# Adaptive modulation by channel tile, with the first two tiles of h in three pieces

## What is computed

```python
def rms_norm(x, g):
    xf = x.astype(jnp.float32)
    y = xf * lax.rsqrt(jnp.mean(xf * xf, axis=-1, keepdims=True) + RMS_EPS)
    return (y * g.astype(jnp.float32)).astype(x.dtype)
...
    c_act = jax.nn.silu(c)
...
        mod = (c_act @ w_ada[l] + b_ada[l])[:, None, :]
        shift, scale, gate = jnp.split(mod, 3, axis=-1)
        h = rms_norm(x, g_norm[l]) * (1 + scale) + shift
        proj = h @ w_in[l]
...
        x = x + gate * (m @ w_out[l])
```

## Time and profile before

| | us |
|---|---|
| median of 3 runs (918.33 to 919.73) | 918.34 |
| span of the profiled execution | 917.1 |
| TensorE busy | 902.9 (98%) |
| VectorE busy | 797.5 (87%) |
| ScalarE busy | 414.1 (45%) |
| GpSimd busy | 100.7 (11%) |

### The profile page before, as it was taken

The page is one execution under the profiler, slowest core; times in us unless marked ns, Lnnn a source line. Parts: engine busy times, 40 slices in busy tenths (PEclk is TensorE's granted clock), DMA queues, the critical chain, the costliest instruction groups (busy, mean ns, idle before and its releaser), DMA issues.

```text
span 917.1 us, 17124 instructions
## 1 busy us (share of the span) xinstructions
PE 902.9 (98%) x7004; PEld 884.6 (96%) x7004; DVE 797.5 (87%) x915; ACT 414.1 (45%) x582; POOL 100.7 (11%) x109
## 2 busy tenths in 40 slices
PE   8999999999999999999999999999999999999996
PEld 5699999999999999999999999999999989999996
DVE  1797999997999996999997799999798798689767
ACT  5484354434453443454433445446434432436452
POOL 0122211111110201211111203000011000000000
PEclk9999999999999999999999999999999999999998
DMA  9879989889798979798888989648897662522515
GB/s 367 348 175 224 258 207 255 226 224 245 200 227 248 256 236 236 195 249 243 250 253 251 229 234 226 201 139 291 350 343 184 194 252 90 155 74 92 164 68 185
DMA packets 86366, 202.75 MB, mean 221 GB/s; under 512 B 12433, under 2 KB 19089, under 8 KB 82833
## 3 DMA queue, kind: packets, MB, share of 16 engines
q1 hardware_dynamic: 52960, 122.76, 38.7%
q0 software_dynamic: 22080, 52.46, 28.5%
q10 hardware_dynamic: 11248, 26.45, 8.1%
HBM read 175.67 MB, written 88.88 MB: 288 GB/s over the span
## 4 chain that ended last, share of the span: by engine, by line
PE 95%; DMA 2%; DVE 1%; SPq 1%; issue 0%; ACT 0%; DVEq 0%
PE ps L1080 23%; PE ps L1076 23%; PE ps L1074 23%; PE ps L1011 8%; PE ps L1014 8%; PE ps L1012 8%; DMA ada_raw<-w_ada 2%; PE ps L941 1%; PE ps L993 1%; PE ps L947 0%; PE ps L1272 0%; PE ps L1270 0%; PE ps L1269 0%; DVE bf L1821 0%; DVE hf L2374 0%
## 5 line engine op out<-in xcount | busy, mean ns | idle before, releaser
L2012 DVE SCALAR_TENSOR_TENSOR conv_y<-conv_u,par_all,conv_y 128x1024 f32<-128x1024 f32 x240 | 301.1, 1284 | 2.1 <-DVE conv_y L1998 0.6
L1076 PE MATMUL ps<-tr,hr 128*128 128x258 f32 x824 | 216.4, 283 | 0.0
L1074 PE MATMUL ps<-tr,hr 128*128 128x258 f32 x824 | 215.4, 283 | 0.0
L1466 ACT ACTIVATE hr<-raw 128x512 fp32r<-128x512 f32 (+1 forms) x188 | 115.9, 618 | 116.1 <-PE ps L1080 87.5
L1080 PE MATMUL ps<-tr,hr 128*128 128x258 f32 x824 | 166.4, 283 | 0.0
L1076 PE MATMUL ps<-hr 128*128 128x258 f32 x616 | 161.5, 283 | 0.0
L1074 PE MATMUL ps<-hr 128*128 128x258 f32 x616 | 160.8, 282 | 0.0
L1074 PEld LDWEIGHTS ps<-tr,hr 128*128 128x128 f32 x824 | 156.9, 190 | 0.0
L1076 PEld LDWEIGHTS ps<-tr,hr 128*128 128x128 f32 x824 | 155.7, 189 | 0.0
L1891 DVE TENSOR_TENSOR hr<-raw,hr 128x512 fp32r<-128x512 f32 (+1 forms) x188 | 126.5, 677 | 5.5 <-ACT hr L1466 1.6
L1080 PEld LDWEIGHTS ps<-tr,hr 128*128 128x128 f32 x824 | 127.3, 188 | 0.0
(11 more groups left out here) (289 smaller groups left out, 1581.5 us busy)
## 6 DMA issues: line engine op xcount, KB each, us to landing
w_sums<-w_main POOLq DMA_DIRECT2D x64, 512.0 KB, 9.5
raw<-w_sums SPq DMA_DIRECT2D x120, 256.0 KB, 4.5
raw<-w_main SPq DMA_DIRECT2D x94, 256.0 KB, 4.8
w_sums<-w_sums POOLq DMA_DIRECT2D x30, 512.0 KB, 5.8
w_sums<-w_main ACTq DMA_DIRECT2D x26, 512.0 KB, 5.5
ada_raw<-w_ada SPq DMA_DIRECT2D x8, 1024.0 KB, 21.1
w_raw<-w_main SPq DMA_DIRECT2D x16, 512.0 KB, 5.7
bf<-x_t SPq DMA_DIRECT2D x4, 1032.0 KB, 8.1
```

What stands on the lines that cost most here:

```text
L1074: nc.tensor.matmul(bank[:, c, :], wh[:, w_cols], x_hi[:, k, t_cols], start=start and k == 0, stop=False, skip_group_check=True)
L1076: nc.tensor.matmul(bank[:, c, :], wh[:, w_cols], x_lo[:, k, t_cols], start=False, stop=False, skip_group_check=True)
L1466: nc.scalar.activation(ring(q)[0][:, 0:n], raw5[:, raw_slot(q), 0:n], ACT.Copy).then_inc(item_hi, 1)
L2012: ins = v.scalar_tensor_tensor(out=y, in0=conv_u[:, x, k:k + SEQ], scalar=par_all[:, g, x, k:k + 1], in1=y, op0=ALU.mult, op1=ALU.add)
```

## The change

- **Modulation by tile.** w_ada's shift and scale columns are stored as 8 blocks of 256 columns, one for each channel tile (the gate's two blocks become the tensor w_gate). There are 8 products, 8 row copies of 256 columns and 8 turns of two matmuls, in place of 4 of each of double size. VectorE's modulation is two instructions of 9 columns, straight from the PSUM bank, and uses scale_b = (1 + b_scale) * g_norm, which is made once at the start.
- **Squares.** ScalarE squares tiles 0, 2, 4, 6 and half of 7, VectorE tiles 1, 3, 5 and the other half. TensorE sums eight strips of 129 columns on eight groups of 16 rows, so that the root and the reciprocal have 129 columns in place of 258. The last two tiles of x are loaded apart.
- **h.** VectorE first multiplies x by the spread 1/rms in place (x_norm; from tile 2 on x_norm_row with the copied row), ScalarE then makes the full h with scale and shift (h_full) and copies it to the high part (h_hi), and VectorE subtracts (h_lo, a plain subtraction). Tiles 0 and 1 go in pieces of 387, 387 and 258 columns, and TensorE's step of job 0 on them waits for piece after piece (split_step).
- **Order.** c's SiLU and its table come at ScalarE's start. The first w_ada block and its product come before the first weights and the spreading. Jobs 0 and 1 go in turn for 6 tiles in place of 5. Fewer spare matmuls.

```diff
-QCOLS = TOK // QUADS
+PIECES = 2 * QUADS
+PCOLS = TOK // PIECES
+PIECE_BANKS = [(0, 3), (3, 6), (6, PIECES)]
+H_PIECES = [slice(p0 * PCOLS, p1 * PCOLS) for p0, p1 in PIECE_BANKS]
+SPLIT_TILES = 2
-WARM_SPREAD = 5
+WARM_SPREAD = 3
-WARM_TURN = 3
-WARM_FIRST = 4
+WARM_TURN = 1
...
-            for n in range(4):
-                sp.dma_start(bf[:, 2 * n:2 * n + 2, :], t["x_t"][:, 2 * n:2 * n + 2, :]).then_inc(x_loaded[n], 16)
+            for n, rows in enumerate([slice(0, 2), slice(2, 4), slice(4, 6), slice(6, 7), slice(7, 8)]):
+                sp.dma_start(bf[:, rows, :], t["x_t"][:, rows, :]).then_inc(x_loaded[n], 16)
...
+            for e in range(1, KT):
+                sp.dma_start(ada_raw[:, e, :, :], t["w_ada"][e]).then_inc(ada_loaded[e - 1], 16)
...
-            together = KT - 3
+            together = KT - 2
...
+            for k in range(2, together):
+                first_steps(k, [0])
+                if k + 2 < KT - 1:
+                    turn(k + 2)
+                if k + 3 < KT:
+                    ada(k + 3)
+                first_steps(k, [1])
+                if k == KH:
+                    turn(KT - 1)
...
+            for e in range(1, KT, 2):
+                dve.wait_ge(x_loaded[x_load(e)], 16)
+                columns = slice(HALF, TOK) if e == KT - 1 else slice(0, TOK)
+                v.tensor_tensor(hf[:, e, columns], bf[:, e, columns], bf[:, e, columns], ALU.mult).then_inc(x_squared_dve, 1)
+                if e == 1:
+                    dve.wait_ge(small_loaded, 64)
+                    link(v.scalar_tensor_tensor(out=scale_b.rearrange("p (q x) -> p q x", x=2), in0=ada_b[:, 0:PAIRS, 2:4], scalar=1.0,
+                                                in1=vecs[:, G_NORM, :].rearrange("p (q x) -> p q x", x=2), op0=ALU.add, op1=ALU.mult))
...
+            for e in range(1, KT):
+                modulation(e)
+                h_samples(e)
+                if e + 1 < KT:
+                    x_norm_row(e + 1)
+                h_lo(e)
+                if e == 3:
+                    first_split(0, 1)
+                    first_split(1, 1)
```

More of the change, by code:

```diff
@@ new lines, in square_sums @@
+            def square_sums(e):
+                for h in range(2):
+                    picked = pick_half[:, h * QUAD // 2:h * QUAD // 2 + QUAD]
+                    for g in range(QUADS):
+                        quad = slice(g * QUAD, (g + 1) * QUAD)
+                        p = 2 * g + h
+                        last = nc.tensor.matmul(x_sums[quad, :], picked, hf[:, e, p * PCOLS:(p + 1) * PCOLS], start=(e == 0 and h == 0),
+                                                stop=(e == KT - 1 and h == 1), tile_position=(0, g * QUAD))
+                return last
@@ L991, in token_sums, with spread_rstd @@
+            def spread_rstd(b):
+                p0, p1 = PIECE_BANKS[b]
+                for p in range(p0, p1):
+                    row = p * QUAD // 2
+                    last = nc.tensor.matmul(rstd_bank[b][:, (p - p0) * PCOLS:(p - p0 + 1) * PCOLS], eye[:, row:row + 1].broadcast_to([P, P]),
+                                            x_rstd, start=True, stop=True)
+                last.then_inc(x_spread, 1)
             def token_sums(out, row, done):
@@ L1424, in _ @@
+            h_full(1, 0)
+            ada_out(2)
+            h_full(1, 1)
+            h_hi(1, 0)
+            h_full(1, 2)
+            h_hi(1, 1)
+            h_hi(1, 2)
+            ada_out(3)
+            for e in range(SPLIT_TILES, KT):
+                h_full(e, 0)
+                h_hi(e, 0)
+                if e + 2 < KT:
+                    ada_out(e + 2)
+                if e == 3:
                     first_split(0, 1)
                     first_split(1, 1)
-                if e % 2 == 1 and e > 1:
-                    h_full(e - 3)
-                    h_full(e - 2)
@@ L1429, in _ @@
-            h_full(KT - 2)
-            h_full(KT - 1)
             def evac_first(s):
@@ L1833, in _ @@
[L1833 to L1841 removed]
+            for b in range(len(H_PIECES)):
+                x_norm(1, b)
+            for e in range(1, KT):
[4 more added lines that the diff above has]
+                h_lo(e)
+                if e == 3:
```

311 lines of the change are left out of this document (172 added, 139 removed).

## The result

The changed kernel takes 927.7 us (median of 4 runs, 925.4 to 930.0) where the kernel before takes 918.6 on the same chip (4 runs, 918.3 to 919.7): a ratio of 1.0091, with a 95% interval of 1.0069 to 1.0113. It is slower, by 8.4 us by the ratio (9.1 by the medians), with an interval of 6.3 to 10.4. The forecast was 926.0 in a range of 921.0 to 929.6. The profiled execution is the slowest of the four; its own time is 930.0 and its span 928.2. The spans of the four are 928.2, 924.5, 923.6 and 927.3, 925.9 on the mean, against 925.1 in the sum.

A forecast was written before the change was run, and what follows sets the result against it. TensorE's stream was taken to bound the kernel: span 917.1 + 5.5 (job 2's shift) + 2.5 (clock) = 925.1 us, plus 1.2 from span to median, 926.3, given as 926.0. Range 921.0 to 929.6.

The forecast's parts named there:

- Part 1: Squares: VectorE waits for the small tensors, eye at 13.7 us, holding later squares and TensorE's sums; +3.55 us.
- Part 2: From root to first step: halved columns and pieces start the first step at 28.5 us, 2.9 earlier than before.
- Part 3: Tiles of h: a chain between VectorE and ScalarE takes 3.9 us a tile; TensorE waits 2.5 us before step 7.
- Part 4: Ahead of job 2: TensorE waits 1.4 us for VectorE's weight split; job 2 at 67.05, shift +5.5 us without the clock.
- Part 5: TensorE's clock falls to half at idle gaps ahead of sum 3, the first step and around step 7; +2.5 us, bounds 0 and 4.9.
- a sign of being wrong: TensorE showing a wait behind 70 us that it didn't have before would prove the prediction wrong.
- the measure: Start of job 2, 61.55 us before: its shift was taken as the shift of the whole kernel.
- The clock holds: Rival: no half-clock stretch ahead of or behind sum 3; 923.8 us, or 923.0 with h_full at 1.15; chance 0.17.
- VectorE isn't held: Rival: eye lands before tile 3's square needs it, sums keep their old pace; some 919.8 us; chance 0.05.
- The ring is shorter: Rival: a tile of h takes 3.2 us or less, so TensorE's steps alone bind; 917.1 us; chance 0.04.
- Both together: Rival: VectorE isn't held and the ring is shorter than TensorE's need; 913.6 us; chance 0.03.
- The pieces do nothing: Rival: the first step waits for the whole tile, starting 1.1 us later, but time stays at 926; chance 0.05.

The follow-up runs named there:

- both spares: Changed kernel plus 16 spare matmuls behind the sum of tile 2 and 5 ahead of the first step; 925.5 us, ratio 1.0069.
- first kernel above: Changed kernel with the wait for the small tensors and scale_b moved behind VectorE's last square; 922.9 us, ratio 1.0039.
- all edits and the five spares: The kernel with all edits plus five spare matmuls ahead of the first step; 917.2 us, ratio 0.9974.
- the ring opened: Changed kernel with VectorE's modulation of the next tile moved ahead of this tile's low part; 924.6 us, ratio 1.0057.
- all edits: Changed kernel with scale_b and its wait behind squares, next modulation before h_lo, weight split before t3, sigmoid table loaded early; 917.3 us, ratio 0.9976.
- the sixteen: Changed kernel plus 16 spare matmuls behind the sum of tile 2, where TensorE waits for square 3; 927.5 us, ratio 1.0083.
- both edits: Changed kernel with scale_b and its wait behind the squares and the next tile's modulation ahead of h_lo; 919.6 us, ratio 1.0004.
- without the pieces: The kernel with all edits, but first steps of tiles 0 and 1 wait for the whole tile; 920.1 us, ratio 0.9998.

## Why the prediction was right, and where it was off

The forecast case came true: slower, through all three of its terms. That the number, 926.0, lies so near the 927.7 is in part luck, as several errors cancel. Point by point:

**Part 1, the hold.** Right, and the largest term. eye was put at 13.7 and landed by 14.05, 0.35 late, within its bounds of 13.6 and 14.6. Square 3 was put at 13.95 and started at 14.25. The bare term was put at 3.55 us; with the clock up it is 3.9, from a root at 16.40 without the hold to one at 20.32 with it and both spares. In the changed kernel's trace it is 6.1 (22.49), the other 2.2 being the clock. In the medians all of it comes to 4.8.

**Part 2, root to first step.** Right to 0.5 us: 8.65 forecast from the end of the sums to the first step, 8.21 measured. The pieces gave what they were to give: the first step waits for the first piece only, and the second costs 0.2.

**Part 3, the ring.** 3.92 a tile forecast; 3.91 and 3.92 measured from one low part to the next from tile 2 on, but for the tile with the weight splits. The number is better than its working: the terms as they stand there (0.3, 1.23, 1.06, 1.23 and 0.2) add up to 4.02. In the trace the four starts are 0.39, 1.28, 1.10 and 1.15 us apart (57.38, 57.77, 59.05, 60.15, 61.30), 3.92 in all. Over six tiles the 0.1 would have been 0.6 us. Nor does 1.15 in place of 1.23 for h_full take 0.85 us off, as Part 4 has it, but over six tiles some 0.5. The wait ahead of step 7 was put at 2.5 and is 2.23. The price of h_full, taken from a row of another stage, 1.23, is 1.24 here. That the ring hides under TensorE before tile 7 holds: from tile 1 on, the one wait ahead of an earlier step is 0.33 us (at 53.69). With the clock up, h_lo(7) comes 0.7 us earlier than the 61.3 of the forecast (step 7 at 60.62), since modulation 1 starts 0.35 earlier and tile 1 takes 4.2 us from there and not 4.7.

**Part 4, job 2's weights.** The size is right, the name only in part. From step 7 to job 2 the forecast has 5.75 us; with the clock up it is 5.81 and the split ends last (first kernel above), but in the changed kernel and in the one with both spares it is 6.54, and ScalarE's evacuation ends last. Behind job 0 ScalarE has the high part 1.06, the table 1.28 and the sigmoid 1.03 in a row, here in the first kernel above:

```profile
59.70 1.06 ACT L1433 ACTIVATE w_hi<-w_raw 128x1024 fp32r<-128x1024 f32 x1 [3.05 <-PE ps L1050]
60.78 1.28 ACT L1517 ACT_TABLE_LOAD   x1
62.08 1.03 ACT L1517 ACTIVATE stage_hi<-ps 128x1032 f32<-128x1032 f32 x1
```

The high part starts 1.73 us after step 7 (57.97), and the sigmoid ends 0.6 ahead of the split. TensorE's wait there, put at 1.4, is 1.28 in this kernel and 0.55 in the changed one. With step 7 at half clock ScalarE starts 2.99 us after it (68.33 after 65.34), 1.3 later, and ends 0.6 behind the split; job 2 is later by 0.7. I had looked at VectorE's queue behind the low part, and not at ScalarE's behind job 0, though the trace of before has this evacuation end at 61.08, only 0.2 ahead of the split. That the kernel with both spares hits 67.05 so closely is owed to two errors that cancel, the 0.7 too late at step 7 and the 0.7 too early from there; and its first step hits 28.5 because the sums end 0.4 later than forecast and Part 2 is shorter by as much.

**Part 5, the clock.** The mechanism is right and the size off. The length of a stretch was read from a window that cuts off its start: the one before is 3.4 us and not 3.05. Of the three stretches the first two were 6.8 us long, and the second cost not a part but the most: from the first step to step 7 are 34.7 us, against 32.15 with the clock up, 2.55 us. The first made the three gaps between sums 1.75 in place of 0.99, 2.3 us. The third cost 0.7. Their sum is 5.6 in the profiled execution, above my upper bound of 4.9, though by the medians only some 2.7 (2.0, with its noise, by the kernel with both spares, and 0.7 for the third). I had +2.5. So the median met the forecast, in part by luck, while the profiled execution's span lies 3 us above the 925.1 of the sum.

**Behind 70 us** I had nothing. 0.8 us were lost there, 0.4 of it in a wait that before didn't have (L1024 for VectorE's stage_hi), which the prediction had named as a sign of being wrong. It touches the measure, the start of job 2, whose shift was to be the shift of the whole: in the ten traces of other kernels than before the span comes out up to 1.9 us later than job 2's shift says, 1.9 in the one with all edits and the five spares.

**The rivals.** "The clock holds" put the kernel at 923.8; with both early stretches taken away it is at 925.5, and its trace has 1.2 in a wait in the items and 0.7 for the stretch at step 7, which stayed. "VectorE isn't held" was put at 919.8; the kernel in which it isn't gives 922.9, in part for a chip on which the kernel before takes 919.5, and then for two losses: job 2 starts 0.3 to 1.1 us later than the rival had it, behind a stretch of 3.4 us at half clock in the first tiles, and 1.4 us go behind it, 0.8 of them in one wait. "The ring is shorter" gave 917.1; opened, and with the hold left in, it gives 924.6. Both together were put at 913.6 and gave 919.6: with the two causes gone, job 2's own wait of 1.28 us, which that rival had taken to vanish, is still there, TensorE needs 34.1 us without it from first step to job 2 where the rival has 31.8, and the item stream gives some back. So even with the ring opened TensorE's own need was put too low; 0.65 of the 2.3 us are two waits for h, and the rest was not taken apart. "The pieces do nothing" had them worth nothing in the time, since modulation 1 stands behind h_lo(0) in any case. Where the ring no longer binds, they are worth 2.0 to 2.8 us, probably for the most part through the idle time that they cut. In the changed kernel itself that wasn't tried.

## What to carry to other kernels

A wait on an in-order engine holds all that stands behind it, so a step that needs late data (here 8 columns of constants) goes behind the work that doesn't need it. A chain that goes back and forth between two engines costs the round trip for each tile, and not the work of the busier engine: issuing the next tile's modulation before this tile's subtraction took the last round of the ring from 3.9 to 2.7 us. An earlier first step is worth only what stays of it: here 2.6 of 6.8 us were work that had moved behind it. Price an idle place of TensorE not only by its length but by what runs at half clock behind it, the small matmuls that feed other engines included, and close all such places together: closing one of three left the other two falls where they were and the median unmoved. Where one engine's queue ends last at a hand-over, look at what ends 0.6 us before it on the other, or the fix will show nothing.

## What the runs showed of the hardware

**Stretches at half clock have two lengths here.** In the first 75 us of the traces they are 3.4 or 3.5 us long (among them those at 27.7 in the kernel before, 25.8 with the wait moved, 30.4 with the ring opened, 26.2 with all edits, 60.5 with both spares, 63.2 with the sixteen, 65.1 in the changed kernel), or 6.8, as in the changed kernel twice, at idle times of 3.7 and 1.9 us. Nearly the same idle time ahead of the first step was followed by different ones: 1.92 us by 6.8 us at half clock in the changed kernel, 1.93 by 3.4 with the ring opened, 1.82 by 3.4 in the kernel with all edits, 1.61 by none with both edits, and 2.97 by none in the profile without the pieces. So the length of the idle time alone doesn't decide it. That it differs from run to run of one kernel is likely, and would account for runs that spread over 4 us and go with their mean granted clock; but only one execution of each kernel was profiled. The Trainium skill (TensorE: Matmul & The Clock Gate, HAM oscillation) describes the pattern, idle time between bursts and each burst starting at the low clock; the windows of the changed kernel at 14.0, 31.1 and 65.2 us agree with it, and the 2.97 us without a fall don't.

**Small transfers of a second queue come one after each load of the first.** With the last load of x cut in two, eye landed at 14.05, 11.1 us after its issue; before, with that load whole, at 14.6. The small tensors before it landed at 5.9, 8.5, 11.1 and 13.7 us before, and the four loads of x at some 5.7, 8.3, 10.9 and 13.5, one small tensor 0.1 to 0.3 us behind each. With the cut the last of them came half a microsecond earlier, of the 0.9 that Part 1 had; no run changes the cut alone.

**The item stream has single waits that differ from kernel to kernel.** Between job 2's start and the matmul that waits for tok_rstd the kernel before takes 847.7 us. The others take 847.7 to 849.2: 847.7 with all edits, 848.0 with both, 848.5 in the changed kernel and in the one with all edits and the five spares, 848.9 with the wait moved, 849.2 with both spares. Where it is more than 0.3, single waits make up half of it or more, as this one of the kernel with both spares, its longest behind 66 us:

```profile
PE ps L1139 <- ACT u L1621: 1.2, 1, 1.2
```

They stand at different places, and behind the stream up to 1.1 us more go to matmuls at half clock. Neither was taken apart: what ScalarE or VectorE was late for there, and whether it is the order in which transfers meet, stays open. It bounds what this study can say of differences under 2 us.
